# Expert 0's rows selected from contiguous columns, and matrices loaded chunk by chunk, in a hybrid backbone with routed experts

## The chip, the cores and the metric

One core of a Trainium2 chip runs the whole program. The metric is the time of one execution on the device in microseconds. The engines are named as in the profile: PE (TensorE, with PEld for its weight loads), DVE (VectorE), ACT (ScalarE), POOL (GpSimd) and SP (SyncE, which here only issues DMAs).

## What is computed

A step of a two-layer backbone for 512 sample tokens and 128 prompt tokens of width 1024. Each layer has a mixer with an output projection, a residual sum, a norm, and then a mixture of 16 experts, in which each expert chooses its tokens: 64 of the samples and 16 of the prompts. What matters here, with `norm` for the scaled norm and its modulation, and `x` the residual stream after the mixer:

```python
def ec_moe(x, router_w, w_gate, w_up, w_down):
    bsz, n_tok, _ = x.shape
    cap = n_tok * EC_CAPACITY // N_EXPERTS
    aff = jax.nn.softmax(jnp.einsum('btd,de->bte', x, router_w).astype(jnp.float32), axis=-1)
    gate, idx = lax.top_k(jnp.swapaxes(aff, 1, 2), cap)
    bidx = jnp.arange(bsz)[:, None, None]
    xe = x[bidx, idx]
    hid = jax.nn.silu(jnp.einsum('becd,edf->becf', xe, w_gate)) * jnp.einsum('becd,edf->becf', xe, w_up)
    ye = jnp.einsum('becf,efd->becd', hid, w_down) * gate[..., None].astype(x.dtype)
    return jnp.zeros_like(x).at[bidx, idx].add(ye)
```

In a layer: `x = x + g1 * out`, then `x = x + g2 * ec_moe(norm(x), ...)`. All is fp32. An expert has three matrices of 2 MB, so a layer reads 96 MB of weights.

## The kernel before

The kernel writes out the order of each engine by hand, in blocks; inside a block the engines meet at counting semaphores. `out_and_route` makes the block at issue for either layer, `experts` gives its second part. SBUF is full, so the same places are used by stages in turn.

**Output projection.** `product(t, h)` multiplies token tile t (tiles 0 to 3 are samples, PT = 4 is the prompts) by half h of the projection's 1024 columns. Each operand is split into a high and a low part of rounded fp32, so that a chunk k of the 8 chunks of the inner dimension takes three matmuls of 128x512 (L1663 to L1665). The high parts of the weights lie in `wv_high`, ring blocks 2 and 3, the low ones in `wv_low`, blocks 0 and 1. DVE adds the residual (L1730, L1732), ACT and DVE make the norm's factor `rstd`, and SP stores each tile of x and of the normed x in DRAM (L1638, L1640).

**Weights of the experts.** A matrix is loaded in four parts of 512 KB by `load_weights` (L1404) into one of ten slots, `wraw`, of which `SLOT_AT` tells the places. `EXPERT_ORDER` gives the order: gate 0, up 0, gate 1, up 1, down 0, gate 2, up 2, down 1 and so on, 48 matrices. The first three lie in places that are free early. Slots 3 to 6 are the four ring blocks, which the projection reads to its end. SP waits for its last product (`mm` at 10), issues matrices 3, 4 and 5, then waits for the logits and issues 6 and 7, then for the selection and issues 8, and last for the row stores and issues 9. From matrix 10 on, SP waits until the slot's former matrix is used up.

**Routing.** PE turns x (L1675) and multiplies it by the router (L1456). DVE makes the softmax and finds the eight largest of each row again and again (L1506 to L1509). PE turns the chosen slots (L1715, L1718), DVE merges the halves (L1755 to L1762) and gives the 64 token numbers of expert 0 as a column, `slot_of`. PE spreads it over the partitions (L1543), and DVE makes of it four matrices `pick` (L1809): 1 times the norm's factor where a token of tile t is the chosen one.

**Expert 0's rows.** The later experts fetch their rows by indirect DMAs on POOL (L1929, L1920). Expert 0's are made by matmuls from x in SBUF. `tensor_choice` multiplies each `pick` by x, with the columns regrouped: `columns` takes every eighth column, so that the chunk of rows that a transpose must turn lies together. Two column groups go to two array tiles of 64 columns (L1548), on which they make PSUM partitions 0 to 63 and 64 to 127. ACT copies the 128x512 sum (L2097), PE turns it with four transposes (L1971), ACT and DVE scale and shift it (L2066, L2134), and `first_hidden` multiplies chunk after chunk by the gate and up matrix (L1957 on four tiles of 32 columns). Between its chunks it does the prompts' choice (L1565 to L1567), the selection of the prompts' rows (L1558), and their turning (L1990). `keep_busy` (L143) are matmuls of the identity into a bank that nobody reads, between the selection and what follows.

**The other experts.** `into_hidden` (L1957, L1963), `turn_hidden` (L2023), `turn` (L1945) and `down` follow for each expert, and `down` waits for the weighing of the expert before (L2161, L2166). The last expert of layer 0 shares its time with what the next layer needs: `sync_last` issues three loads of its projection, `scalar_last` splits them on ACT (L2314) before ACT copies the last expert's weighed rows (L2120).

## Time and profile before

| | |
|---|---|
| median of 3 runs | 1416.8 us (1416.03 to 1419.14) |
| the profiled execution | 1415.48 us |
| its span, first to last instruction | 1413.6 us |
| mean granted TensorE clock | 0.982 |
| PE busy | 1324.3 us (94%) |
| DVE, ACT, POOL busy | 698.1, 529.4, 276.8 us |
| DMA | 333.80 MB; in the expert stages 369 to 388 GB/s in most slices |
| expert stage of layer 0 | about 443 to 741 us |
| expert stage of layer 1 | about 1098 to 1401 us |

The time is that of an execution as the host sees the device; the span leaves out what lies before the first and behind the last instruction. Each row of a timeline merges instructions of one form that follow each other. An fp32 matmul of the program is two rows of PE in the profile, two passes; a transpose is one. Ends of matmuls are modelled, so starts are the better clock, and a group's time is from its first start to its last end. A load's part in the landing time is not all transfer, since it queues behind what was issued before.

### The profile page before, as it was taken

How to read it: one execution, taken by the hardware profiler on the slowest of the kernel's cores; microseconds unless marked ns; L12 is line 12 of the kernel's file. 1: busy time of each engine (PE TensorE's matmuls, PEld its weight loads, DVE VectorE, ACT ScalarE, POOL GpSimd, SP SyncE). 2: the span in 40 equal slices, each digit the busy share in tenths (PEclk: the TensorE clock that was granted, in tenths of full speed). 3: DMA queues.
4: the chain of work that ended last, by engine and by line, in shares of the span. 5: the costliest groups of instructions: out<-in, count | busy, mean ns of one | idle time of the engine just before them, and what ended most of it. 6: DMA issues, size and time to landing. Idle time of an engine off the chain costs nothing. (4 is left out here: it accounts for less than half of the span.)

```text
span 1413.6 us, 27174 instructions
## 1 busy us (share of the span) xinstructions
PE 1324.3 (94%) x11105; PEld 806.2 (57%) x11105; DVE 698.1 (49%) x1636; ACT 529.4 (37%) x1221; POOL 276.8 (20%) x237
## 2 busy tenths in 40 slices
PE   5999998889899999999989999989899999999995
PEld 1756566766686444444438998555588444444443
DVE  1536514677635333344357628866735344333435
ACT  2723113676333322222225468665523322222213
POOL 0001104596002011111100040555301011111101
PEclk7999999999999999999999999999999999999997
DMA  9688860131437999999982022050053999999985
GB/s 364 232 327 333 331 217 25 37 144 46 182 119 258 369 374 374 375 374 376 388 294 77 4 69 60 1 223 1 14 225 112 373 378 376 374 375 379 374 312 179
DMA packets 105799, 333.80 MB, mean 236 GB/s; under 512 B 23182, under 2 KB 29164, under 8 KB 99532
## 3 DMA queue, kind: packets, MB, share of 16 engines
q1 hardware_dynamic: 99276, 310.11, 57.9%
q0 software_dynamic: 5824, 19.86, 6.0%
q8 instruction: 88, 1.44, 0.4%
q10 hardware_dynamic: 576, 2.10, 0.4%
q14 instruction: 35, 0.29, 0.1%
HBM read 308.13 MB, written 23.89 MB: 235 GB/s over the span
## 5 line engine op out<-in xcount | busy, mean ns | idle before, releaser
L1957 PE MATMUL psum<-wraw,proj 128*32 128x512 f32 x3072 | 403.0, 598 | 7.7 <-issue 6.0
L1963 PE MATMUL psum<-wraw,proj 128*16 128x256 f32 x3072 | 235.6, 381 | 0.6 <-ACT proj L2071 0.6
L1963 PEld LDWEIGHTS psum<-wraw,proj 128*16 128x16 f32 x3072 | 90.2, 97 | 232.2 <-issue 227.4
L1957 PEld LDWEIGHTS psum<-wraw,proj 128*32 128x32 f32 x3072 | 96.8, 110 | 79.7 <-issue 15.8
L1925 POOL DMA_INDIRECT x_rows<-modrow,idx x30 | 42.9, 1429 | 452.6 <-DVE modrow L2166 452.6
L2084 ACT ACTIVATE proj<-psum 128x320 f32<-128x320 f32 x32 | 14.0, 437 | 286.5 <-PE psum L2023 286.5
L2128 DVE TENSOR_SCALAR proj<-psum,proj 128x64 f32<-128x64 f32 x232 | 55.6, 312 | 107.0 <-PE psum L1945 107.0
L1336 POOL TENSOR_SCALAR ring<-ring,small 128x640 f32<-128x640 f32 x48 | 90.3, 1886 | 39.8 <-DVE small L1275 39.4
L2161 DVE SCALAR_TENSOR_TENSOR modrow<-psum,proj 64x512 f32<-64x512 f32 x60 | 45.0, 749 | 84.2 <-PE psum L1963 83.8
L2153 DVE TENSOR_TENSOR proj<-proj,psum 64x512 f32<-64x512 f32 x32 | 22.1, 690 | 127.5 <-ACT proj L2091 127.5
L1266 DVE TENSOR_REDUCE small<-psum 128x1 f32<-128x640 f32 (+1 forms) x80 | 57.3, 717 | 52.3 <-PE psum L1241 51.8
L421 PE MATMUL psum<-ring_rounded,xT_rounded 128*128 128x512 f32 (+1 forms) x200 | 76.6, 383 | 3.4 <-DVE xr_rounded L638 3.4
L423 PE MATMUL psum<-ring_rounded,xr_rounded 128*128 128x512 f32 (+1 forms) x200 | 74.0, 370 | 0.0
L422 PE MATMUL psum<-ring_rounded,xT_rounded 128*128 128x512 f32 (+1 forms) x200 | 73.9, 370 | 0.0
L2060 ACT ACTIVATE proj<-psum,proj 128x64 f32<-128x64 f32 x232 | 67.6, 398 | 16.3 <-PE psum L1945 16.1
L1663 PE MATMUL psum<-ring_rounded,proj_rounded 128*128 128x512 f32 x160 | 66.8, 418 | 1.8 <-DVE xT_rounded L1766 1.5
L1665 PE MATMUL psum<-ring_rounded,xT_rounded 128*128 128x512 f32 x160 | 64.4, 403 | 0.0
L1664 PE MATMUL psum<-ring_rounded,proj_rounded 128*128 128x512 f32 x160 | 64.1, 401 | 0.0
L1310 ACT ACTIVATE ring<-psum,small 128x640 f32<-128x640 f32 x64 | 50.9, 795 | 24.9 <-DVE small L1269 20.8
L2166 DVE SCALAR_TENSOR_TENSOR modrow<-psum,proj 16x256 f32<-16x256 f32 x120 | 57.8, 482 | 1.8
L2091 ACT ACTIVATE proj<-psum 64x512 f32<-64x512 f32 x32 | 18.8, 589 | 101.5 <-PE psum L1963 101.5
L1210 PE MATMUL psum<-ident,ring 128*128 128x128 f32 x320 | 46.3, 275 | 9.6 <-POOL ring L1336 7.0
(519 smaller groups left out, 2410.6 us busy)
## 6 DMA issues: line engine op xcount, KB each, us to landing
wraw<-in_exp_w_gate_dram SPq DMA_DIRECT2D x128, 512.0 KB, 16.4
wraw<-in_exp_w_up_dram SPq DMA_DIRECT2D x128, 512.0 KB, 16.8
wraw<-in_exp_w_down_dram SPq DMA_DIRECT2D x128, 512.0 KB, 16.5
ring<-in_ada_w_dram SPq DMA_DIRECT2D x29, 1024.0 KB, 6.9
hold<-in_ada_w_dram SPq DMA_DIRECT2D x14, 1024.0 KB, 6.8
ring<-in_ev_w_in_dram SPq DMA_DIRECT2D x4, 2048.0 KB, 12.3
xr<-x_rows SPq DMA_DIRECT2D x15, 512.0 KB, 7.5
proj<-in_ada_w_dram SPq DMA_DIRECT2D x5, 1024.0 KB, 9.1
```

The lines of the kernel that those rows point to most:

```text
L421: pe.matmul(bank(n % UB, w), xTh[:, k, tok], mv[:, k, :], start=(k == 0), stop=False)
L422: pe.matmul(bank(n % UB, w), xTh[:, k, tok], mv_low[:, k, :], start=False, stop=False)
L423: mm = pe.matmul(bank(n % UB, w), xTl[:, t, k, :], mv[:, k, :], start=False, stop=(k == KD - 1))
L1266: own.link(dve.tensor_reduce(mx[:, i % NB:i % NB + 1], scores(i), AX.XY if wide[i] else AX.X, ALU.max))
L1336: pool.tensor_scalar(Pb[u % NB][:, 0:w], Pb[u % NB][:, 0:w], rr[:, u % NB:u % NB + 1], None, ALU.mult).then_inc(s["n"], 1)
L1663: pe.matmul(bank(u % 4), xh[:, t % 2, k, :], wv_high[:, k, cut], start=(at == 0), stop=False)
L1664: pe.matmul(bank(u % 4), xh[:, t % 2, k, :], wv_low[:, k, cut], start=False, stop=False)
L1665: mm = pe.matmul(bank(u % 4), x_low, wv_high[:, k, cut], start=False, stop=(at == KD - 1))
L1957: mm = pe.matmul(psum[quad(q, 32), b, :], xs[:, quad(q % 2, 32)], pair[q // 2], start=first, stop=last)
L1963: mm = pe.matmul(psum[quad(q, CAPP), b, 0:QP], xs[:, CAPS:CAP], pair[q // 2][:, q % 2 * QP:(q % 2 + 1) * QP], start=first, stop=last)
L2060: ins = act.activation(xgT[:, e % 2, k, lo:hi], bank(0)[:, k * CAP + lo:k * CAP + hi], ACT.Identity, scale=scale_of[:, c, k:k + 1], bias=s ...
L2166: return dve.scalar_tensor_tensor(out=y[CAPS:CAP, q * QP:(q + 1) * QP], in0=psum[rows, 4, 0:QP], scalar=gd[rows, 1, e:e + 1], in1=g2p[rows ...
```

## The change

Three things change.

1. **The selection.** It takes contiguous columns of x. The two array tiles take two token tiles each (0 and 1; 2 and 3) in place of two groups of columns, for one half of the 1024 columns and then for the other, in two PSUM banks. Each tile thus has a sum over half of the samples. PE waits for all four picks first.
2. **The turning.** ACT copies each half's sums when they are ready. A product with `both_halves`, the upper and lower half of the identity side by side and summed (128x64), adds the two halves of the samples and turns the rows in one: eight fp32 products, of every eighth column as weights, into banks 5 and 6. The modulations read from there. The order of the chunks follows the banks. The prompts' sums go to bank 1 and the prompts' slots to bank 7.
3. **The loads.** The last product, now `last_product`, takes the chunks 4 to 7 first and tells after each chunk that it is done. After chunk i SP issues one part of each of two matrices (`free_chunk`): parts 0 to 3 of matrices 3 and 4 after the first four chunks, those of 5 and 6 after the last four. For that the slots of 4, 5 and 6 exchange their ring blocks. The last tile's store of the normed x is issued behind the parts of the first two chunks. The third load for the next layer waits for 47 matrices used and not 46, since its place is now that of matrix 46.

The diff, cut to its core:

```diff
-        SLOT_AT = [("ring", 4 * 4096), ("ring", 5 * 4096), ("proj", PROJ_SLOT), ("ring", 3 * 4096), ("ring", 2 * 4096), ("ring", 0), ("ring", 4096),
+        SLOT_AT = [("ring", 4 * 4096), ("ring", 5 * 4096), ("proj", PROJ_SLOT), ("ring", 3 * 4096), ("ring", 4096), ("ring", 2 * 4096), ("ring", 0),
...
                 sp.wait_ge(s["st"], 16 * ST)
-                load_weights(sp, l, 6, ready)
                 load_weights(sp, l, 7, ready)
-                sp.wait_ge(selected, 1)
+                sp.wait_ge(selected, 2)
...
                 keep_busy(pe, 2, 5)
-                for t in range(ST):
-                    pe.wait_ge(s["pick"], t + 1)
-                    for c in range(2):
-                        mm = pe.matmul(psum[64 * c:64 * c + CAPS, 1, :], pick[:, t, :], columns(t, 4 * c, 4 * c + 4), start=(t == 0), stop=(t == ST - 1))
-                    if t == ST - 2:
-                        turn_affinities(pe, 1)
-                mm.then_inc(selected, 1)
-                keep_busy(pe, 5, 5)
+                pe.wait_ge(s["pick"], ST)
+                for h in range(2):
+                    for j in range(2):
+                        for c in range(2):
+                            t = 2 * c + j
+                            mm = pe.matmul(psum[64 * c:64 * c + CAPS, h, :], pick[:, t, :], xr[:, t, h * 512:(h + 1) * 512], start=(j == 0), stop=(j == 1))
+                        if h == 1 and j == 0:
+                            turn_affinities(pe, 1)
+                    mm.then_inc(selected, 1)
+                keep_busy(pe, 5, 4)
+
+            def tensor_rows(pe, rows):
+
+                for k in range(KD):
+                    at = k // 2 * CAPS
+                    mm = pe.matmul(bank(5 + k % 2)[:, at:at + CAPS], rows[:, k::KD], both_halves, start=True, stop=True)
+                return mm
...
+            LAST_ORDER = (4, 5, 6, 7, 0, 1, 2, 3)
+
+            def free_chunk(sp, i):
+
+                sp.wait_ge(s["chunk"], i + 1)
+                for m in (3, 4) if i < 4 else (5, 6):
+                    load_part(sp, l, m, ready, i % 4)
...
                         sp.dma_start(x_rows[t * P:(t + 1) * P, :], xr[:, t, :]).then_inc(s["st"], 16)
+                        if t == ST - 1:
+                            for i in range(2):
+                                free_chunk(sp, i)
                         sp.wait_ge(s["xm"], t + 1)
                         sp.dma_start(xm_rows[t * P:(t + 1) * P, :], xm[:, t % 2, :]).then_inc(s[f"row{t % 2}"], 16)
-                    sp.wait_ge(s["mm"], 2 * TILES)
-                    load_weights(sp, l, 3, ready)
-                    load_weights(sp, l, 4, ready)
-                    load_weights(sp, l, 5, ready)
+                    for i in range(2, KD):
+                        free_chunk(sp, i)
...
+                    def last_product():
+
+                        b = bank((2 * PT + 1) % 4)
+                        pe.wait_ge(s["gx"], 2 * PT - 2)
+                        for at, k in enumerate(LAST_ORDER):
+                            pe.matmul(b, xh[:, PT % 2, k, :], wv_high[:, k, 512:], start=(at == 0), stop=False)
+                            pe.matmul(b, xh[:, PT % 2, k, :], wv_low[:, k, 512:], start=False, stop=False)
+                            mm = pe.matmul(b, xT_r[:, k * NT + PT * P:k * NT + (PT + 1) * P], wv_high[:, k, 512:], start=False, stop=(at == KD - 1))
+                            mm.then_inc(s["chunk"], 1)
...
+                            own(dve.tensor_tensor(both_halves, ident[:, 0:CAPS], ident[:, CAPS:2 * CAPS], ALU.add))
...
-                    pe.wait_ge(s["selc"], 1)
-                    for k in range(4):
-                        mm = pe.transpose(bank(k // 2)[:, k % 2 * P:(k % 2 + 1) * P], picked_s[:, k, :], ident[:, :])
-                    mm.then_inc(s["xT"], 2)
+                    pe.wait_ge(s["selc"], 2)
+                    routed["tensor_rows"](pe, picked_s).then_inc(s["xT"], 2)
...
-                act.wait_ge(s["sel"], 1)
-                act.activation(picked_s, bank(1).rearrange("p (k d) -> p k d", k=4), ACT.Copy).then_inc(s["selc"], 1)
+                for h in range(2):
+                    act.wait_ge(s["sel"], h + 1)
+                    act.activation(picked_s[:, h * 512:(h + 1) * 512], bank(h), ACT.Copy).then_inc(s["selc"], 1)
...
-                for i, used in enumerate((41, 43, 46)):
+                for i, used in enumerate((41, 43, 47)):
```

How the selection stands in PE's order, before (a row counts the program's matmuls, of 128 partitions of `xr` by 64 columns of picks into 64x512 sums; waits are left out):

```order
L143 MATMUL psum<-ident 128x128 x2
L1548 MATMUL psum<-xr,proj 64x512 x6
L1465 MATMUL psum<-ident,proj 16x128
L1548 MATMUL psum<-xr,proj 64x512 x2
L143 MATMUL psum<-ident 128x128 x5
L1971 MATMUL psum<-ident,proj 128x128 x4
```

and as the change has it:

```order
L143 MATMUL psum<-ident 128x128 x2
L1554 MATMUL psum<-xr,proj 64x512 x6
L1468 MATMUL psum<-ident,proj 16x128
L1554 MATMUL psum<-xr,proj 64x512 x2
L143 MATMUL psum<-ident 128x128 x5
L1564 MATMUL psum<-small,proj 128x64 x8
```

The selection keeps its 8 matmuls and its fillers; the four transposes became eight products.

On SP's queue in layer 0, from the last tile's stores on, before (wraw_61 is slot 3, wraw_64 slot 6):

```order
L1638 DMA x_rows<-xr 128x1024
L1640 DMA xm_rows<-xm 128x1024
L1404 DMA wraw_61<-in_exp_w_up_dram 128x1024 x4
L1404 DMA wraw_62<-in_exp_w_down_dram 128x1024 x4
L1404 DMA wraw_63<-in_exp_w_gate_dram 128x1024 x4
L1404 DMA wraw_64<-in_exp_w_up_dram 128x1024 x4
```

and as the change has it:

```order
L1658 DMA x_rows<-xr 128x1024
L1402 DMA wraw_61<-in_exp_w_up_dram 128x1024
L1402 DMA wraw_62<-in_exp_w_down_dram 128x1024
L1402 DMA wraw_61<-in_exp_w_up_dram 128x1024
L1402 DMA wraw_62<-in_exp_w_down_dram 128x1024
L1663 DMA xm_rows<-xm 128x1024
L1402 DMA wraw_61<-in_exp_w_up_dram 128x1024
L1402 DMA wraw_62<-in_exp_w_down_dram 128x1024
```

The store of the last normed tile stands behind four parts; the parts of two matrices alternate, and those of slots 5 and 6 follow in the same way.

## Rows read from the trace of the kernel before

**Rows 1.** Timeline, PE, one row an expert: start us, us, line, op, tiles, count.

```profile
679.34 0.71 PE L2023 MATMUL psum<-ident,proj 80*128 80x80 f32 x4
...
697.22 0.70 PE L2023 MATMUL psum<-ident,proj 80*128 80x80 f32 x4
```

**Rows 2.** The same in layer 1.

```profile
1334.78 0.71 PE L2023 MATMUL psum<-ident,proj 80*128 80x80 f32 x4
...
1351.93 0.71 PE L2023 MATMUL psum<-ident,proj 80*128 80x80 f32 x4
```

**Rows 3.** Waits of PE, 640 to 700 us: total, times, longest.

```profile
PE psum L1957 <- DMA wraw<-in_exp_w_up_dram: 0.5, 1, 0.5
```

**Rows 4.** Windows: PE, PEld, DVE, ACT, POOL busy, clock, DMA share, GB/s.

```profile
430.00:434.00 4.00, 4.00 (x20) 3.23 (x19) 3.72 (x15) 0.00 (x0) 1.78 (x2) 1.00 0.00 0
```

**Rows 5.** Timeline, SP's DMA issues, layer 0.

```profile
422.06 0.32 SPq L1640 DMA_DIRECT2D xm_rows<-xm  x1
434.00 1.76 SPq L1404 DMA_DIRECT2D wraw<-in_exp_w_up_dram  x4
```

**Rows 6.** Timeline, ACT: copies out of PSUM.

```profile
428.42 0.60 ACT L1855 ACTIVATE proj<-psum 128x512 f32<-128x512 f32 x1 [1.00 <-PE psum L1665]
434.01 0.60 ACT L1855 ACTIVATE proj<-psum 128x512 f32<-128x512 f32 x1 [4.99 <-PE psum L1665]
```

**Rows 7.** Timeline, PE, from the selection to the first expert product.

```profile
443.64 5.71 PE L1548 MATMUL psum<-xr,proj 128*64 128x512 f32 x12
...
449.49 2.03 PE L1548 MATMUL psum<-xr,proj 128*64 128x512 f32 x4
451.45 1.38 PE L143 MATMUL psum<-ident 128*128 128x128 f32 x10
452.67 0.60 PE L1971 MATMUL psum<-ident,proj 128*128 128x128 f32 x4
453.86 0.64 PE L1957 MATMUL psum<-wraw,proj 128*32 128x512 f32 x4 [0.59 <-ACT proj L2066]
```

**Rows 8.** Timeline, DVE: the four picks.

```profile
443.18 1.10 DVE L1809 TENSOR_SCALAR proj<-psum,small 128x64 f32<-128x64 f32 x4 [1.14 <-PE psum L1543]
```

**Rows 9.** Timeline, PE: groups that price one pass, layer 0.

```profile
438.27 1.04 PE L1675 MATMUL psum<-ident,xr 128*128 128x128 f32 x8
...
456.34 2.78 PE L1957 MATMUL psum<-wraw,proj 128*32 128x512 f32 x24
458.94 1.10 PE L1558 MATMUL psum<-xr,proj 128*32 128x256 f32 x8
...
463.40 1.92 PE L1963 MATMUL psum<-wraw,proj 128*16 128x256 f32 x32 [0.28 <-ACT proj L2071]
465.26 1.09 PE L1945 MATMUL psum<-ident,proj 64*128 64x64 f32 x8
```

**Rows 10.** Timeline, PE: two 64-column tiles, contiguous.

```profile
308.34 1.08 PE L1223 MATMUL psum<-proj 128*64 128x256 f32 x8
```

**Rows 11.** Timeline, PE: fp32 products with 128 columns of weights.

```profile
750.16 1.95 PE L2440 MATMUL psum<-small,xr 128*128 128x128 f32 x16
```

**Rows 12.** Timeline, POOL: gather of expert 1.

```profile
442.87 1.12 POOL L1929 DMA_INDIRECT proj<-xm_rows,idx  x1 [5.57 <-DVE idx L1762]
```

**Rows 13.** DMA issues, 440 to 470 us: KB each, median us to landing.

```profile
xm_rows<-xm ACTq DMA_DIRECT2D x1, 512.0 KB, 8.2
...
proj<-xm_rows,idx POOLq DMA_INDIRECT x3, 7.4
```

**Rows 14.** Timeline, ACT: what follows the last expert of layer 0.

```profile
731.22 7.04 ACT L2314 ACTIVATE ring_rounded<-ring 128x832 fp32r<-128x832 f32 x8 [4.58 <-DMA ring<-in_od_w_in_dram]
739.45 0.63 ACT L2120 ACTIVATE ring_rounded<-ring 80x512 fp32r<-80x512 f32 x1 [1.18 <-DVE ring L2161]
```

**Rows 15.** Windows with a lowered TensorE clock.

```profile
390.00:395.00 5.00, 5.00 (x18) 4.03 (x18) 0.98 (x3) 1.93 (x4) 0.00 (x0) 0.66 0.00 0
...
729.20:734.30 5.10, 5.10 (x33) 1.68 (x37) 2.73 (x7) 3.08 (x4) 1.40 (x1) 0.50 0.69 155
```

More of the change, by code:

```diff
@@ L1395, in build, with load_part, load_weights @@
         PARTS = 4
-        def load_weights(sp, l, m, ready):
+        def load_part(sp, l, m, ready, i):
             n, e = EXPERT_ORDER[m]
             src = A[EXPERT_W[n]][l, e].rearrange("(p k) n -> p (k n)", p=P)
-            parts = PARTS
-            w = 4096 // parts
-            for i in range(parts):
-                sp.dma_start(wraw[m % NSLOT][:, i * w:(i + 1) * w], src[:, i * w:(i + 1) * w]).then_inc(ready[m % NSLOT], 16)
+            w = 4096 // PARTS
+            sp.dma_start(wraw[m % NSLOT][:, i * w:(i + 1) * w], src[:, i * w:(i + 1) * w]).then_inc(ready[m % NSLOT], 16)
+        def load_weights(sp, l, m, ready):
+            for i in range(PARTS):
+                load_part(sp, l, m, ready, i)
         def landed(m):
@@ L1446, in out_and_route @@
             token_of, slot_of = small[:, 48:48 + TILES], small[0:CAPS, 56:57]
+            both_halves = small[:, 64:64 + CAPS]
             ssq, rstd, mxs, sums = small[:, 0:5], small[:, 8:13], small[:, 16:21], small[:, 24:29]
@@ L1557, in tensor_prompts @@
                 for q in range(4):
-                    mm = pe.matmul(psum[32 * q:32 * q + 2 * CAPP, 3, 0:256], pick_p, columns(PT, 2 * q, 2 * q + 2), start=True, stop=True)
+                    mm = pe.matmul(psum[32 * q:32 * q + 2 * CAPP, 1, 0:256], pick_p, columns(PT, 2 * q, 2 * q + 2), start=True, stop=True)
                 mm.then_inc(selected, 1)
@@ L1563, in tensor_chosen @@
                 for e in range(2):
-                    at = CAPS + CAPP * e
-                    pe.matmul(spread[:, at:at + CAPP], ident[0:NE, e:e + 1].to_broadcast([NE, P]), idxf[0:NE, CAPS:CAP], start=True, stop=True)
+                    pe.matmul(spread_p[:, e * CAPP:(e + 1) * CAPP], ident[0:NE, e:e + 1].to_broadcast([NE, P]), idxf[0:NE, CAPS:CAP], start=True, stop=True)
                 pe.transpose(bank(7)[0:CAP, 0:NE], idxf[0:NE, :], ident[0:NE, 0:NE])
@@ L1591, in vector_chosen @@
                 dve.wait_ge(s["it"], 4)
-                dve.tensor_scalar(pick_p, spread[:, CAPS:CAPS + 2 * CAPP], token_of[:, PT:TILES], rstd[:, PT:TILES], ALU.is_equal, ALU.mult).then_inc(s["pick"], 1)
+                dve.tensor_scalar(pick_p, spread_p, token_of[:, PT:TILES], rstd[:, PT:TILES], ALU.is_equal, ALU.mult).then_inc(s["pick"], 1)
                 dve.tensor_copy(idx[CAPS:CAP, :], bank(7)[CAPS:CAP, 0:NE]).then_inc(s["chosen"], 1)
@@ L1708, in _ @@
                     product(PT, 0, 7, KD)
-                    product(PT, 1)
+                    last_product()
                     keep_busy(pe, 20, 3)
@@ L1808, in _ @@
                     for t in range(ST):
-                        dve.tensor_scalar(pick[:, t, :], spread[:, 0:CAPS], token_of[:, t:t + 1], rstd[:, t:t + 1], ALU.is_equal, ALU.mult).then_inc(s["pick"], 1)
+                        dve.tensor_scalar(pick[:, t, :], spread, token_of[:, t:t + 1], rstd[:, t:t + 1], ALU.is_equal, ALU.mult).then_inc(s["pick"], 1)
                     then["vector"](dve, own)
@@ L1829, in turn_copy @@
                             act.wait_ge(s["turned"], 2 * t + h + 1)
-                            if h == 0:
+                            if h == 0 and t < PT:
                                 act.wait_ge(s["mm"], 2 * t + 2)
@@ L1975, in first_hidden @@
                     pairs = [[wraw[m][:, k * 512:(k + 1) * 512] for m in (0, 1)] for k in range(KD)]
-                    for n, k in enumerate((0, 4, 1, 5, 2, 6, 3, 7)):
+                    for n, k in enumerate((0, 2, 4, 6, 1, 3, 5, 7)):
                         if n < 3:
@@ L1987, in first_hidden @@
                         if n == 7:
-                            pe.wait_ge(s["selc"], 2)
+                            pe.wait_ge(s["selc"], 3)
                             for j in range(2):
-                                mm = pe.transpose(bank(j)[:, 0:P], picked_p[:, j, :], ident[:, :])
+                                mm = pe.transpose(bank(5 + j)[:, 0:P], picked_p[:, j, :], ident[:, :])
                             mm.then_inc(s["xT"], 2)
@@ L2183, in vector @@
                 dve.wait_ge(s["xT"], 2)
-                for k in (2, 6, 3):
+                for k in (1, 3, 5):
                     modulate_picked(k)
```

33 lines of the change are left out of this document (19 added, 14 removed).

## The prediction

> **What bounds the kernel now.** I read the windows of busy time and clock first, then the timeline of PE, then that of SP and the waits. In both expert stages PE has no idle window, and one expert takes 17.15 us from one turn of hidden rows to the next [rows 2]. PE sets the pace there: a stage begins with the first expert's products and ends 16 experts later. Once it doesn't. In layer 0 the step to expert 15 took 697.22 - 679.34 = 17.88 us [rows 1], 0.73 us more, and in that stretch PE waits for a DMA, an up matrix [rows 3]: the weight stream has just run out of lead. It is a second bound right behind the first, and a change that starts PE earlier gains only if the stream starts earlier too.
>
> The stream stands still before the stage: DMA share 0.00 from 430 to 434 us [rows 4]. SP, done with its last row store at 422.06, waits for the very last product and issues the fourth matrix at 434.00 [rows 5]. That product is the half that runs between the two PSUM copies, 428.42 to 434.01 [rows 6]: 5.59 us for 8 chunks, 0.70 each. What the first expert waits for is the selection: its matmuls begin at 443.64, filler at 451.45, the transposes at 452.67, the first expert product at 453.86 [rows 7].
>
> **Part one, the selection.** Before, it is 8 matmuls of 512 columns, two passes each, on two 64-column tiles side by side: 8 paired passes, from 443.64 to 451.45, 7.81 us [rows 7]. The moving operand steps 8 floats. Six pairs are listed with 5.71 us and the last two with 2.03, so a further pair costs (5.71 - 2.03) / 4 = 0.92 us, and 7.81 - 8 x 0.92 = 0.45 us go to the affinities' transpose among them and to the end. Afterwards it is again 8 paired passes, of contiguous columns. Price of one: four tiles do 24 contiguous passes of 512, six groups of four, in 2.78 us [rows 9], and one group by itself takes 0.64 [rows 7], so (2.78 - 0.64) / 5 = 0.43 us. Two 64-column tiles do four pairs of 256 contiguous columns in 1.08 us [rows 10], at most 0.27 a pair, so 0.54 for 512 is the upper end. It is the step of 8 floats that costs the double, not the tiles: four tiles take 1.10 us for 8 strided passes of 256, and 1.92 us for 32 contiguous ones, 0.48 for 8 [rows 9]. So 8 x 0.43 + 0.45 = 3.89 us, which is -3.92 (upper end -3.0).
>
> The change waits for all four picks before the first matmul. DVE makes four in 1.10 us [rows 8]. PE started 443.64 - 443.18 = 0.46 after their start, so it starts at least 1.10 - 0.46 = 0.64 later, and at most 1.10 less a quarter, 0.82; I take 0.76, since PE needs a little to hear of a pick. The affinities' transpose comes nearer to the picks, behind six paired passes, 2.6 us after the start. DVE makes the softmax that it needs right behind the picks, with seven operations on 16 columns and one exponent on ACT; it held nothing before, and I put it at 0.
>
> **Part two, the turning.** Four transposes (0.60 us [rows 7]) become 8 fp32 products with 128 weight columns and 64 moving ones, 16 passes. Such a group of 16 takes 1.95 us with contiguous weights [rows 11]. Here the weights step 8 floats. Low end: transposes of such weights take 1.09 us for 8, contiguous ones 1.04 [rows 9], a factor of 1.05. High end: the factor 1.10 / 0.48 = 2.3 that the moving operand paid, 4.5 us. I take 1.95, since a strided weight load is nearest to a strided weight load. +1.35 us; at the high end +3.9.
>
> The Trainium skill speaks against this part: page "SBUF — State Buffer", its passage on 16-byte cachelines, lets fp32 step by 4 elements at full rate and charges beyond, and it makes no exception for weights. By it the sum would be the first rival's, by the rows it is mine.
>
> The selected rows were copied once, 128x512 as in [rows 6], 0.60 us. Now the first half is copied while PE still multiplies, and the second takes the same 0.60 under the five fillers (1.38 us [rows 7]): 0. The modulations, the prompts' selection and their waits keep number and form and change banks: 0. The DVE addition that makes the summed identity is one small operation while PE multiplies without a gap: 0, and 0.2 us without that cover.
>
> A layer: -3.92 + 0.76 + 1.35 = -1.81 us; first product at 452.05.
>
> **Part three, the stream.** Chunk 1 of the last product ends at 428.4 + 0.7 = 429.1, so the fourth matrix starts 434.0 - 429.1 = 4.9 us earlier. On SP's queue the last row store moves from 422.06, idle DMA time, behind four parts of 512 KB: 512 KB more in the stream, at the page's 375 GB/s 1.4 us. Net lead +3.5 us. Layer 0 needs 1.81 + 0.73 = 2.54 us of it for PE to run through; the lead suffices by 1.0, and the 0.73 us go too. Layer 1 had no such wait. More lead is worth nothing: PE's pace holds.
>
> Who waits for the moved store? POOL's gather for expert 1, at 442.87 [rows 12]. Four issues take SP 1.76 us [rows 5], so the store is issued at about 430.9, and with the 8.2 us that one took amid traffic [rows 13] it lands at 439.1. Cover is left: 3.8 us, and after the gather's 7.4 us [rows 13] still 12 us until PE turns these rows at 465.26 [rows 9]. The third load for the next layer now waits for one down product more, about 5 us; ACT waits for it before it copies the last rows, after 731.22 + 7.04 = 738.26, with 1.18 us to spare [rows 14], and has the new lead. 0; without the lead about 1 us, once.
>
> **Sum.** 2 x -1.81 - 0.73 = -4.35 us. The profiled execution took 1415.5 us, with a span of 1413.6; it would be 1411.1. The median of the runs shown lies 1.3 us above it, and I forecast that: **1412.4 us**.
>
> **Rivals.** (1) *The strided weights pay* in full: 4.5 us instead of 1.95, so a layer gains -1.81 + 2.55 = +0.74; the wait in layer 0 still goes: 1416.8 + 1.5 - 0.7 = 1417.6, no change. Against it stand 1.09 and 1.04 [rows 9]; for it, that those were transposes of 64 rows and not products of 128. 11%.
> (2) *The stream comes no earlier where it counts*, because parts issued two by two and the store among them are served worse. At a lead of 0, PE gains nothing in layer 0 and under 1 us in layer 1: 1416. For it: [rows 3] shows the lead exhausted. Against: the DMAs stand quite still for 4 us [rows 4]. 8%.
> (3) *Slower, by the clock.* PE now stands about 0.7 us before the selection. The granted clock was 0.66 in 390 to 395, though PE was busy, and 0.50 in 729.2 to 734.3, after PE had stood for 3 us [rows 15]. Those 5.1 us of work at 1.2 GHz cost 2.6. One such fall a layer gives 1412.4 + 5.1 = 1417.5; it decides from 3.6 us lost a layer (2 x 3.6 - 4.35 = +2.8), and two falls, at the picks and at the copy, give 1412.4 + 10.2 = 1422.6. Against: PE stood 0.59 us before the first product [rows 7] without a fall there. One 4%, two 4%.
> (4) *More than forecast*: the 1.3 us between median and profiled run are waits for weights too, and go with the new lead: 1411.1 or less. 12%.
>
> **The numbers.** My own case has 59% and reaches from 1411.2 to 1414.0 (one bound of the selection or a quarter of the weights' price). 0.2%, 2.8 us, is about what a measurement of this kernel can tell from no change: below 1414.0 is faster. Faster: 59 + 12 + 2 of rival 2 = 0.73. Same: 11 + 6 + 4 = 0.21. Slower: 4 and 2 for what I don't see = 0.06. The range, 1410.2 to 1416.2, takes in part of rival 2 and half of rival 1's price, and leaves out their far ends and the clock.
>
> **What would show it.** The selection 3.9 us long; the turning 1.9 to 2.0 us for 16 passes; the first expert product 8.9 us after the picks start (before 453.86 - 443.18 = 10.7); the DMAs busy from 430 us; no expert of layer 0 at 17.9 us, all at 17.15. The forecast is wrong if the turning takes over 3 us, if PE waits for a weight DMA anywhere, if the granted clock around 444 us is under 1, or if more went than these two places show.

## The result: slower, and by how much

| | before | after |
|---|---|---|
| median of the runs | 1416.4 us (6 runs, 1414.1 to 1419.1) | 1427.0 us (6 runs, 1423.6 to 1430.0) |
| profiled execution, its span | 1415.5, 1413.6 us | 1424.7, 1422.9 us |
| mean granted TensorE clock of the profiled execution | 0.982 | 0.973 |
| the same over the runs | 0.980 (23 runs) | 0.970 (6 runs) |

The ratio is 1.0067, with a 95% interval of 1.0049 to 1.0085. The forecast was 1412.4 us, in a range of 1410.2 to 1416.2. The result is 10.6 us slower than before, outside the range, and on the side that I had given 6%.

### The profile page after: what moved, and what is told of

Read it like the earlier page. It is cut to its first block and busy times, and to the rows that moved or that the text cites. A ratio compares the mean times of both kernels' runs of the same rounds, so it can differ in the third digit from the quotient of the medians.

```text
span 1422.9 us, 27224 instructions
## 1 busy us (share of the span) xinstructions
PE 1336.5 (94%) x11129; PEld 818.9 (58%) x11129; DVE 698.2 (49%) x1638; ACT 529.5 (37%) x1223; POOL 276.4 (19%) x237
## 5 line engine op out<-in xcount | busy, mean ns | idle before, releaser
L1684 PE MATMUL psum<-ring_rounded,proj_rounded 128*128 128x512 f32 x144 | 59.8, 416 | 1.8 <-DVE xT_rounded L1797 1.5
L1686 PE MATMUL psum<-ring_rounded,xT_rounded 128*128 128x512 f32 x144 | 57.6, 400 | 0.0
L1685 PE MATMUL psum<-ring_rounded,proj_rounded 128*128 128x512 f32 x144 | 57.1, 397 | 0.0
```

Of the source, the lines that this page charges most:

```text
L1684: pe.matmul(bank(u % 4), xh[:, t % 2, k, :], wv_high[:, k, cut], start=(at == 0), stop=False)
L1685: pe.matmul(bank(u % 4), xh[:, t % 2, k, :], wv_low[:, k, cut], start=False, stop=False)
L1686: mm = pe.matmul(bank(u % 4), x_low, wv_high[:, k, cut], start=False, stop=(at == KD - 1))
```

## The profile after

I read the windows of the changed stretch first: from the first matmul of the selection to the first one of the prompts' rows, in layer 0 and layer 1. The columns are those of [rows 4]: the stretch, the busy time of PE, PEld, DVE, ACT and POOL with their instructions, the granted clock, the DMA share and GB/s. First the kernel before.

```profile
443.64:458.94 15.30, 14.71 (x79) 4.62 (x82) 5.47 (x27) 3.77 (x9) 1.28 (x2) 1.00 1.03 396
1099.08:1114.38 15.30, 14.71 (x79) 4.62 (x82) 5.47 (x27) 3.77 (x9) 1.08 (x2) 1.00 1.03 392
```

And the changed kernel.

```profile
443.24:461.12 17.88, 17.29 (x90) 8.45 (x93) 4.77 (x24) 4.19 (x9) 0.93 (x1) 0.81 1.03 393
1104.66:1123.67 19.01, 18.42 (x89) 8.90 (x93) 4.77 (x24) 4.07 (x9) 0.91 (x1) 0.73 1.03 394
```

The forecast made this stretch 2.6 us shorter (-3.92 and +1.35). It became 2.58 us longer in layer 0 and 3.71 in layer 1. Two columns say why. The weight loads (PEld, the second one) are busy for 8.45 and 8.90 us where they were for 4.62. And the granted clock is 0.81 and 0.73 where it was 1.00.

The timeline of PE shows the places (start, length, line, operation, operands, count, and the idle time ahead with what ended it). Layer 0 first, then layer 1.

```profile
443.24 4.49 PE L1554 MATMUL psum<-xr,proj 128*64 128x512 f32 x12 [0.62 <-DVE proj L1841]
...
447.87 1.08 PE L1554 MATMUL psum<-xr,proj 128*64 128x512 f32 x4
...
450.10 3.91 PE L1564 MATMUL psum<-small,proj 128*128 128x64 f32 x16
454.59 3.37 PE L1993 MATMUL psum<-wraw,proj 128*32 128x512 f32 x16 [0.59 <-ACT proj L2100]
...
458.52 2.78 PE L1993 MATMUL psum<-wraw,proj 128*32 128x512 f32 x24
```

```profile
1104.66 2.80 PE L1554 MATMUL psum<-xr,proj 128*64 128x512 f32 x12 [0.62 <-DVE proj L1841]
...
1107.60 1.08 PE L1554 MATMUL psum<-xr,proj 128*64 128x512 f32 x4
...
1109.82 3.96 PE L1564 MATMUL psum<-small,proj 128*128 128x64 f32 x16
1114.38 3.64 PE L1993 MATMUL psum<-wraw,proj 128*32 128x512 f32 x16 [0.59 <-ACT proj L2100]
...
1119.04 4.80 PE L1993 MATMUL psum<-wraw,proj 128*32 128x512 f32 x24
```

In layer 1 the selection runs at full clock. Its 12 and 4 instructions start at 1104.66 and end at 1108.68, 4.0 us, against [rows 7] with 7.8: part one did what was forecast. In layer 0 the same 12 take 4.49 us instead of 2.80, since the clock fell to 1.2 GHz within them. The 16 passes of the turning take 3.91 and 3.96 us in both layers, where 1.95 was forecast from [rows 11]. The first product's rows show the second fall: 16 instructions in 3.37 and 3.64 us, and in layer 1 the 24 behind them in 4.80, where [rows 9] has 2.78. At full clock the 16 take 1.92 us (experiment 1, below). Ahead of both places PE stands idle for a short time: 0.62 us for the picks, which is new, and 0.59 us for the modulated rows, which stood in [rows 7] too, without a fall.

The stream did what was forecast. SP issues the fourth matrix at 428.01 ([rows 5]: 434.00), the DMAs are busy from 430 us ([rows 4]: share 0.00), and the expert that took 17.88 us [rows 1] takes 17.15. Of the 6.0 us between the two issues 1.1 are that this whole execution was ahead there: POOL's addition for the residual, which nobody changed, starts at 428.09 where it was 429.20. That leaves the 4.9 us of the forecast.

```profile
428.01 0.33 SPq L1402 DMA_DIRECT2D wraw<-in_exp_w_up_dram  x1
```

```profile
430.00:434.00 4.00, 4.00 (x25) 3.46 (x24) 3.69 (x14) 0.60 (x1) 1.17 (x2) 1.00 0.99 325
```

```profile
664.37 0.71 PE L2057 MATMUL psum<-ident,proj 80*128 80x80 f32 x4
...
681.52 0.71 PE L2057 MATMUL psum<-ident,proj 80*128 80x80 f32 x4
```

So in the profiled pair the span grows by 9.3 us: 2.58 + 3.71 = 6.3 in the changed stretches, 2 x 0.62 = 1.2 for the waits ahead of them, -0.73 for the stall that is gone. That makes 6.8. The other 2.5 us lie in code that did not change. These are windows of the kernel before and of the changed kernel behind layer 0's experts and in the attention of layer 1.

```profile
740.00:757.00 17.00, 11.76 (x71) 10.33 (x70) 12.15 (x23) 10.73 (x23) 3.35 (x5) 1.00 0.71 210
918.00:945.00 27.00, 22.54 (x119) 15.84 (x117) 16.22 (x47) 17.50 (x41) 14.30 (x9) 1.00 0.75 292
```

```profile
740.00:757.00 17.00, 13.15 (x62) 11.20 (x62) 11.34 (x21) 10.24 (x22) 3.35 (x5) 0.80 0.69 211
918.00:945.00 27.00, 24.05 (x103) 16.76 (x101) 11.23 (x33) 14.39 (x32) 10.15 (x7) 0.75 0.73 287
```

The clock fell there too, to 0.80 and 0.75 on average, though nothing was changed. Whether the change caused that is the question of experiment 5.

## The experiments

Each time stands beside runs of the kernel before on the same chip, whose median was 1415.6 us beside experiments 1 to 4 (23 runs), 1416.7 beside 5 to 8 (35) and 1417.6 beside 9 to 12 (29); a time is compared with its own. Each ratio is uncertain by 0.0013 to 0.0020 either way, which is 2 to 3 us. The stretch named above is what I compare in the profiles, since nearly all that changed lies in it.

**1. Regrouped rows.** The two copies on ScalarE write the chosen rows by their k, so that the turning reads neighbouring columns.

```diff
-                    mm = pe.matmul(bank(5 + k % 2)[:, at:at + CAPS], rows[:, k::KD], both_halves, start=True, stop=True)
+                    mm = pe.matmul(bank(5 + k % 2)[:, at:at + CAPS], rows[:, k * P:(k + 1) * P], both_halves, start=True, stop=True)
...
-                    act.activation(picked_s[:, h * 512:(h + 1) * 512], bank(h), ACT.Copy).then_inc(s["selc"], 1)
+                    act.activation(picked_s.rearrange("p (k d) -> p k d", k=KD)[:, :, h * 64:(h + 1) * 64], bank(h).rearrange("p (d k) -> p k d", k=KD), ACT.Copy).then_inc(s["selc"], 1)
```

> The changed kernel, with ScalarE's two copies writing expert 0's rows regrouped, so that each turning product reads 128 neighbouring columns as weights instead of every eighth. Weights theory (the stride costs the PE about 0.13 us a pass, which made the turning 3.91 and 3.96 us where 1.95 was forecast): the 16 passes take 1.7 to 2.0 us in each layer, two layers give back 4 us, and with all the falls of the clock left as they are the time is about 1423. Rival, the size of the product sets it: the turning stays at 3.9 us and the time at 1427. Rival, the clock: the falls at 444, 454, 744, 925 and 1113 us cost the most (5 to 8 us in all); if they hang on the turning, they go and the time is 1414 to 1418; if not, 1421 to 1425 with falls in the same stages. The regrouped copies should cost the same as before, within 0.1 us; if a strided read of PSUM costs more, the 1.1 us from the last selection matmul to the turning grow.

Measured: 1417.3 us (1414.1 to 1422.4, 11 runs), ratio to before 1.0007 (0.9995 to 1.0020), mean clock 0.975. Its timeline of PE in layer 0:

```profile
446.57 4.49 PE L1554 MATMUL psum<-xr,proj 128*64 128x512 f32 x12 [0.62 <-DVE proj L1841]
...
453.43 1.90 PE L1564 MATMUL psum<-small,proj 128*128 128x64 f32 x16
455.92 1.92 PE L1993 MATMUL psum<-wraw,proj 128*32 128x512 f32 x16 [0.59 <-ACT proj L2100]
```

The turning takes 1.90 us. The weights theory holds: 2.0 us a layer. The stretch, by its windows:

```profile
446.57:460.99 14.42, 13.83 (x89) 6.26 (x93) 4.77 (x24) 4.20 (x9) 0.93 (x1) 0.88 1.03 391
1104.54:1117.26 12.72, 12.13 (x89) 5.93 (x93) 4.77 (x24) 4.09 (x9) 0.91 (x1) 1.00 1.03 387
```

Against the changed kernel it lost 3.46 us in layer 0 and 6.29 in layer 1, together 9.7; the medians, each against its own runs of before, differ by 8.9. 4.0 of that are the stride, the rest is the clock: no fall is left in layer 1, and in layer 0 the one at the selection alone, behind the same 0.62 us of idle time. The copies kept their 0.60 us.

**2. Selection and turning alone**, with the old order of slots and the old loads (the parts of the diff that touch `load_part`, `free_chunk`, `last_product` and `SLOT_AT` undone).

> Parts one and two of the change alone: the new selection and the new turning, with the weights asked for as in the kernel before (whole matrices behind the prompt's last product, the old order of the slots). If the loss comes from the turning and the clock in these parts: slower than before, 1425 to 1430, with the stall of 0.73 us at the twelfth expert of layer 0 there in part or whole, and falls of the clock at the selection. If the asking chunk by chunk is what brought the loss: 1412 to 1416, as my sum for these two parts with a turning of 3.9 us gives it (1416.4 - 3.6 + 4 = 1417).

Measured: 1427.5 us (1421.8 to 1429.7, 6 runs), ratio 1.0075 (1.0058 to 1.0092), mean clock 0.970. The whole loss comes with these two parts. The stretch is the same to 0.03 us as in the changed kernel:

```profile
447.23:465.08 17.85, 17.26 (x89) 8.43 (x93) 4.77 (x24) 4.19 (x9) 0.93 (x1) 0.81 1.03 399
1108.59:1127.60 19.01, 18.43 (x89) 8.89 (x93) 4.76 (x24) 4.07 (x9) 0.91 (x1) 0.73 1.03 398
```

No expert takes over 17.15 us behind the first step in either layer, although the loads are the old ones: PE comes late enough for the stream to keep up. My expectation had the stall still there.

**3. The loads alone**, the counterpart: the old selection and turning.

> Part three alone: matrices 3 to 6 asked for chunk by chunk, the old selection and the old turning. Forecast: the stall of 0.73 us in layer 0 goes and the stream is 5 us ahead, so 1412.5 to 1416. If the asking disturbs something (a queue, the clock in the odd layer at 744 and 925 us): 1419 to 1425 with those falls there and none at the selection.

Measured: 1420.7 us (1415.8 to 1422.7, only 5 runs), ratio 1.0037 (1.0024 to 1.0050), mean clock 0.975. The stall is gone and the stretch takes 15.3 us in both layers, as before, yet the time is above before. I had it repeated, below.

**4. Regrouped rows and fillers.** Experiment 1 with filler products over both idle times.

```diff
-                keep_busy(pe, 2, 5)
+                keep_busy(pe, 5, 5)
...
                     routed["tensor_rows"](pe, picked_s).then_inc(s["xT"], 2)
+                    keep_busy(pe, 3, 4)
```

> As the run with regrouped rows, with three more filler products before the selection (over the 0.62 us in which the PE waits for the picks) and three behind the turning (over the 0.59 us in which it waits for the modulated rows). Clock theory, idle time before a stretch of half-width products makes the clock fall: the falls around 444 and 454 us, and in layer 1 at the same places, are gone, and the time is 3 to 5 us below the run without fillers. Rival, the falls come with the products themselves (64 of 128 columns of the array): they stay, and the time is the same within 1 us. Falls in the odd layer at 744 and 925 us, whose code is unchanged: if they vary from kernel to kernel with no pattern, they are a matter of when the program passes there.

Measured: **1411.0 us** (1407.4 to 1416.4, 12 runs), ratio 0.9962 (0.9946 to 0.9978), mean clock 0.981. It beats the kernel before by 4.6 us, and the changed one, each against its own runs of before, by 15.

```profile
444.31:457.09 12.78, 12.78 (x96) 6.52 (x99) 4.76 (x24) 4.07 (x9) 0.93 (x1) 1.00 1.03 390
1103.44:1116.22 12.78, 12.78 (x96) 6.52 (x99) 4.77 (x24) 4.07 (x9) 0.91 (x1) 1.00 1.03 383
```

The stretch takes 12.78 us in both layers at full clock, 2.52 less than before: the -2.57 of the forecast (-3.92 + 1.35), once the weights are contiguous and the clock stays.

**5. The kernel before, profiled again.**

> The kernel before, unchanged, for a second profile of it and for the clock of more of its executions. Its first profile shows no fall of the clock at 742 and 923 us, where four or five of the others do, on the same code and behind the same idle times (2.46 us at 740, 1.8 us at 921). If these falls come by chance, this profile has one or both and the mean clock of the executions stays at 0.980 (time 1415.6); if they come with the change, this one has none again.

Measured: 1417.7 us (1414.5 to 1425.0, 12 runs), ratio 1.0013 (0.9997 to 1.0029), mean clock 0.979. The profiled execution was one of the longer ones, 1422.9 us, and its windows of the stages with unchanged code read

```profile
740.00:757.00 17.00, 12.23 (x48) 10.20 (x48) 10.28 (x18) 9.51 (x19) 3.35 (x5) 0.70 0.73 216
918.00:945.00 27.00, 24.89 (x112) 17.74 (x110) 9.69 (x27) 14.80 (x32) 8.21 (x6) 0.75 0.66 257
```

with a clock of 0.70 and 0.75. So the falls in those places are not the change's: they come in some executions of the kernel before as well. They go with the spread of single executions of one kernel, up to 10 us, and are why only the changed stretch can be compared between two profiles.

This profile has a fall at the changed place too, though the old selection has no wait of 0.62 us ahead: in layer 1 the clock is low from the fillers on and for the first 2.2 us of the selection. It is the only one among the eight stretches with the old selection (two each of the two profiles of the kernel before and of experiments 3 and 6). It hardly costs: the stretch takes 15.34 us instead of 15.30 and the 12 instructions 5.76 instead of 5.71 [rows 7].

```profile
1106.41:1121.75 15.34, 14.75 (x78) 4.82 (x81) 4.96 (x25) 3.59 (x8) 0.91 (x1) 0.93 1.03 393
```

```profile
1106.41 5.76 PE L1548 MATMUL psum<-xr,proj 128*64 128x512 f32 x12
```

The strided selection takes nearly the same time at either clock, while the contiguous one goes from 2.80 to 4.49 us. Part of what the new selection gains it can therefore lose to a fall that the old one did not feel.

**6. The loads alone, again**, the same kernel as in 3.

> The asking chunk by chunk alone, a second time: the first gave 1420.7 from 5 executions (1415.8 to 1422.7), which at their mean clock of 0.975 is 4 us above the kernel before instead of 3.5 below. If that was the chance of five executions: 1413 to 1416.5 with a clock of 0.979 to 0.980. If the loads do cost clock: 1419 to 1422 at 0.975 again.

Measured: 1418.1 us (1414.2 to 1422.0, 12 runs), ratio 1.0006 (0.9990 to 1.0021), mean clock 0.977. The 5 us of the first run were in part the chance of five executions. What is left is no gain where 0.73 us were forecast for this part alone, which is less than these runs can tell, and a clock slightly under that of before. This stays open, see below.

**7. The changed kernel with the fillers**, its weights still strided (the edit of 4 in the changed kernel).

> The changed kernel with its strided weights, and the six filler products of the run with fillers. The turning stays at 3.9 us (2.0 us a layer over the regrouped rows: 1411.0 + 4.0 = 1415). If the waits alone make the clock fall: no fall within 30 us behind the selection in either layer, 1414 to 1416.5. If the slow turning itself makes it fall: falls behind it at about 454 and 1113 us as in the changed kernel, 1418 to 1422.

Measured: 1418.3 us (1413.8 to 1420.6, 12 runs), ratio 1.0000 (0.9985 to 1.0016), mean clock 0.978.

```profile
445.89:460.69 14.80, 14.80 (x96) 8.54 (x99) 4.77 (x24) 4.08 (x9) 0.93 (x1) 1.00 1.03 384
1101.12:1115.92 14.80, 14.80 (x96) 8.54 (x99) 4.77 (x24) 4.08 (x9) 0.91 (x1) 1.00 1.03 391
```

14.80 us in both layers, without a fall. The slow turning is in there in full (PEld 8.54) and does not bring the clock down by itself. So it needs the waits. Against experiment 4 it is 2.02 us longer in the stretch: the price of the stride again. The median is still 1.8 us above the upper end of what I had expected without a fall.

**8. Regrouped rows and fillers, with the old loads.**

> New selection with regrouped rows and the fillers, but the weights asked for as before (whole matrices behind the last product). With the chunks this kernel took 1411.0. If the chunks are worth what was forecast (3.5 us, the stall of 0.73 us at the twelfth expert of layer 0 among them): 1414 to 1415. If they cost what the run with the chunks alone says (4 us and more): 1405 to 1408. If neither, 1410 to 1412.

Measured: 1418.3 us (1412.7 to 1424.0, 12 runs), ratio 1.0011 (0.9994 to 1.0028), mean clock 0.979. The stretch takes 12.79 us as in 4, but all of it is lost again: PE waits for the up matrices, in layer 0 and then in layer 1 (the waits of PE, total, times, longest), and the steps from 643.53 to 661.05 and on to 679.36 take 17.52 and 18.31 us.

```profile
PE psum L1970 <- DMA wraw<-in_exp_w_up_dram: 2.7, 4, 1.0
```

```profile
PE psum L1970 <- DMA wraw<-in_exp_w_up_dram: 1.7, 3, 0.8
```

```profile
643.53 0.71 PE L2035 MATMUL psum<-ident,proj 80*128 80x80 f32 x4
...
661.05 0.71 PE L2035 MATMUL psum<-ident,proj 80*128 80x80 f32 x4
...
679.36 0.70 PE L2035 MATMUL psum<-ident,proj 80*128 80x80 f32 x4
```

That is the worth of part three: nothing while PE is late, and 6.2 us once the selection is as fast as it should be (1.6 us above its own runs of before here, 4.6 below in experiment 4). I had expected 3.5.

**9 and 10. Fillers ahead of the selection only, and behind the turning only**, both in the changed kernel (one line each of the edit in 4).

> The changed kernel with three more fillers ahead of the selection only, so that the PE does not idle for 0.62 us before it; the strided turning and the 0.59 us behind it stay. With all six fillers the stretch from the selection to the prompts' rows had no fall of the clock and took 14.8 us; without any, 17.9 us (6.8 at the lower clock) and 19.0 us (10.2). If the wait ahead starts the falls and the rest follows from it: no fall in the stretch, 14.7 us in both layers, time 1416 to 1419. If the slow turning with its idle time behind it does so by itself: a fall of 3.4 us or more at the first product in both layers, 16 to 17 us, time 1421 to 1425.

> The counterpart: three fillers behind the turning only; the wait of 0.62 us ahead of the selection stays. If the wait ahead matters by itself: a fall within the selection in layer 0 (at full clock its first 12 instructions take 2.8 us, with the fall 4.5) and none at the first product. If neither: 14.8 us, as with all six. Time 1417 to 1423.

Measured: ahead only 1420.2 us (1414.0 to 1423.4, 12 runs), ratio 1.0013 (0.9995 to 1.0030); behind only 1421.6 us (1415.0 to 1425.8, 12 runs), ratio 1.0024 (1.0004 to 1.0044). The two medians don't tell them apart; the profiles do. Ahead only:

```profile
448.98:463.71 14.73, 14.14 (x90) 7.95 (x93) 4.77 (x24) 4.08 (x9) 0.93 (x1) 1.00 1.03 392
1104.16:1118.89 14.73, 14.14 (x90) 7.95 (x93) 4.77 (x24) 4.08 (x9) 0.91 (x1) 1.00 1.03 393
```

Behind only:

```profile
443.82:461.94 18.12, 18.12 (x95) 9.57 (x99) 4.77 (x24) 4.19 (x9) 0.93 (x1) 0.81 1.03 394
1102.38:1120.51 18.13, 18.13 (x96) 9.31 (x100) 4.77 (x24) 4.19 (x9) 0.91 (x1) 0.81 1.03 394
```

With the picks' wait covered the stretch has no fall, though PE still stands 0.59 us before the first product. With that wait open it has a clock of 0.81 in both layers, though the other is covered. So in these profiles, one of each kernel, it is the 0.62 us ahead of the selection that start the falls, given the slow turning behind; with contiguous weights (experiment 1) the same wait was followed by a fall in one layer of two. My expectation for the second run, that the first product would then be free of a fall, was wrong: its first 16 instructions took 2.96 and 3.16 us instead of 1.92, with filler just ahead of them.

```profile
455.84 2.96 PE L1993 MATMUL psum<-wraw,proj 128*32 128x512 f32 x16
```

```profile
1114.19 3.16 PE L1993 MATMUL psum<-wraw,proj 128*32 128x512 f32 x16
```

The fall at the first product therefore doesn't need the 0.59 us. What goes with it is the slow turning: in layer 0 of experiment 1, with contiguous weights, the fall at the selection is there and the one at the first product is not.

**11. Strides of the weights.** In the kernel before, the 20 fillers ahead of the prompt's turning become 20 products with the normalized rows as weights.

```diff
-                    keep_busy(pe, 20, 3)
+                    for gap in (1, 2, 4, 8):
+                        for n in range(5):
+                            pe.matmul(bank(3, P), xr[:, 0, 0:gap * P:gap], ident[:, :], start=True, stop=True)
```

> The kernel before, with its 20 fillers ahead of the prompt's turning replaced by 20 products of the same size whose weights are columns of the normalized rows at a distance of 1, 2, 4 and 8 elements, five each: it measures the price of the stride by itself. If the price is one of how far apart the 4-byte elements lie: 0.112 us a pass at distance 1, more at 2 and 4, 0.24 us at 8. If it is a step beyond 16 bytes: as at 1 for distances 2 and 4, 0.24 us at 8 alone. If the other operand or the short product made the turning slow: 0.112 us at all four. The time of the kernel stays at 1416 to 1420.

The kernel took 1424.3 us in its one run; the products are 2.6 us longer than the fillers, twice. Windows of that line alone, each over the ten passes of one distance (busy PE, busy PEld, clock, DMA share, GB/s; the counts take in neighbours that overlap):

```profile
432.87:433.98 1.11, 1.11 (x10) 1.11 (x10) 1.00 0.00 0
433.98:435.18 1.20, 1.20 (x12) 1.20 (x11) 1.00 0.83 198
435.18:437.51 2.33, 2.33 (x12) 2.33 (x11) 1.00 1.01 373
437.51:439.91 2.40, 2.40 (x11) 2.37 (x10) 1.00 1.02 374
```

A pass takes 0.111, 0.120, 0.233 and 0.240 us at a distance of 1, 2, 4 and 8 elements, at full clock. None of the three expectations is quite right: it is one step, and it lies between 2 and 4 elements. The DMAs are idle in the first window and busy in the others; that they don't matter is shown by experiment 1, where contiguous passes take 0.11 us at a DMA share of 1.03. The page "SBUF — State Buffer" of the Trainium skill, its passage on 16-byte cachelines, has fp32 step by 4 elements for free; here 4 elements, which is 16 bytes, already pay in full. The same passage wants two hits on each line of 16 bytes for full bandwidth. That rule fits the rows: a distance of 2 still has two elements on a line and 4 has one.

**12. Wait for each pick.** Experiment 4 without the fillers ahead: VectorE makes the picks in the order in which the selection takes them.

```diff
-                keep_busy(pe, 5, 5)
-                pe.wait_ge(s["pick"], ST)
+                keep_busy(pe, 2, 5)
...
+                            if h == 0:
+                                pe.wait_ge(s["pick"], 2 * j + c + 1)
...
-                    for t in range(ST):
+                    for t in (0, 2, 1, 3):
```

> The run with regrouped rows and fillers, without the three fillers ahead of the selection: instead VectorE makes the picks in the order 0, 2, 1, 3 and the selection waits for each as it comes to it. The wait of 0.62 us (0.67 of fillers) should shrink to under 0.1 us in each layer, with no fall of the clock in the selection: 1409.5 to 1411 where that run took 1411.0. If DMAs for the experts' matrices have no slack left, a stall comes back and it stays at 1411; if short waits between the first products let the clock fall: 1412 to 1415.

Measured: 1411.1 us (1410.3 to 1420.7, 12 runs), ratio 0.9961 (0.9942 to 0.9980), mean clock 0.982, like experiment 4. The idle time is gone without filler (no wait for the picks among PE's waits), and the stretch takes 12.98 and 13.86 us:

```profile
443.83:456.81 12.98, 12.98 (x97) 7.23 (x100) 5.47 (x27) 4.25 (x10) 1.28 (x2) 1.00 1.03 388
1095.00:1108.86 13.86, 13.86 (x96) 6.81 (x99) 4.96 (x25) 4.19 (x9) 0.91 (x1) 0.92 1.03 389
```

The 0.92 in layer 1 belongs to a fall that had begun before the selection. The expected gain over experiment 4 is under 1 us and doesn't show in the median.

**13. Transposes against products**, since the row that misled me was one of transposes. The same place as in 11, five groups of four: transposes of 128, 64 and 80 rows, then products of 128 and of 64.

```diff
-                    keep_busy(pe, 20, 3)
+                    for rows, product in ((P, False), (64, False), (80, False), (P, True), (64, True)):
+                        for k in range(4):
+                            w = xr[0:rows, 0, k::KD]
+                            if product:
+                                pe.matmul(bank(3, rows), w, ident[0:rows, 0:rows], start=True, stop=True)
+                            else:
+                                pe.transpose(bank(3, rows), w, ident[0:rows, 0:rows])
```

> The kernel before, its 20 fillers ahead of the prompt's turning replaced by five groups of four, all with weights at a distance of 8 elements (32 bytes): transposes of 128, 64 and 80 rows, then products of 128 and of 64 rows. The experts' rows are turned by transposes of 64 and 80 rows with just this distance at 0.11 us a pass, and that was the row that my forecast trusted. If the kind of instruction decides (a transpose passes its weights once and free of the price): 0.11 us a pass for all three groups of transposes, 0.24 us for both groups of products. If the number of rows decides: 0.24 us for 128 rows, 0.11 us for 64 and 80, whichever the kind. If both: 0.11 us for all but the products of 128 rows.

```profile
433.08 1.78 PE L1716 MATMUL psum<-ident,xr 128*128 128x128 f32 x12
434.70 4.17 PE L1714 MATMUL psum<-ident,xr 128*128 128x128 f32 x16
```

```profile
434.70:436.70 2.00, 2.00 (x8) 1.89 (x8) 1.00 0.97 324
436.70:438.60 1.90, 1.90 (x9) 1.89 (x8) 0.69 1.00 379
```

Its one execution took 1424.9 us, beside one of 1417.0 of the kernel before. The twelve transposes start within 434.70 - 433.08 = 1.62 us, 0.11 each and 0.15 more at each of the two changes of size, whatever the rows; the eight passes of the four products with 128 rows take 2.0 us, 0.24 each and something for the change to the next group. The four of 64 rows need as long a pass, 1.90 us for eight, though part of that is at the lower clock. So the kind of instruction decides: a transpose passes strided weights at full pace, an fp32 product pays.

## Why the prediction was wrong, point by point

- **The selection, -3.92 us a layer: right.** At full clock it takes 4.0 us (3.89 forecast) where it took 7.81.
- **Waiting for all picks, +0.76 us: right in size (0.62 us of idle time), wrong in what it does.** It was priced as time alone. Experiments 9 and 10 show that it starts the falls of the clock: the stretch takes 14.7 us when it is covered and 18.1 when it isn't.
- **The turning, "16 passes at 1.95 us", +1.35: the step that failed first.** The size was 3.91 and 3.96 us, near the high end of 4.5. I chose the low end, "since a strided weight load is nearest to a strided weight load", by the 1.09 and 1.04 us of [rows 9]. Experiment 13 shows what was not alike: those are transposes, these are products, and only products pay. The Trainium skill spoke against this part (page "SBUF — State Buffer", its passage on 16-byte cachelines), and the trace agrees with it at this distance: 0.24 us a pass where contiguous weights take 0.11. It was priced as the first rival, 1417.6 us at 11%.
- **The clock, rival (3), 8%: the step that failed second and costs more.** The mechanism was named with its place, the idle time before the selection, and argued away by the 0.59 us in [rows 7] that had no fall behind them. That was no evidence for the new place: experiment 10 has the new idle time alone and falls in both layers, experiment 9 has the old one alone and doesn't. What tells the two places apart the runs don't show. Experiment 1 shows that the two failed steps are not independent: with contiguous weights only one of the three places with a fall is left. In the changed stretch the clock costs 17.88 - 14.73 = 3.2 us and 19.01 - 14.73 = 4.3 (the 14.73 from experiment 9), near the 2.6 to 5.1 a layer that the rival had.
- **Rivals as alternatives.** The stride and the clock came together: +4.0 and +7.4 us on the 1412.4 make 1423.8. I had priced each alone, and my range took in half of one and nothing of the other. Both hang on the same stretch of PE, so they should have been priced as a pair too.
- **The stream, "4.9 us earlier": right.** 428.01 in place of 434.00, no step of 17.88 us. That PE needs it only if it is early was right as well, and experiments 2 and 8 show both sides of it: no stall with the old loads at a late PE, 5.8 us of longer steps at an early one (3.5 in layer 0, 2.3 in layer 1, all steps together). That layer 1 has no such wait, as I wrote, holds only for the old selection. The store and the gather behind the parts held nobody up.
- **What the sum leaves open.** 1416.4 + 6.3 + 1.2 - 0.7 is 1423.2, and 1427.0 was measured, 3.8 us more. The same sum, each from its own runs of before, leaves 5.1 us over with selection and turning alone (1422.4 against 1427.5), 4.6 with regrouped rows (1412.7 against 1417.3), 5.8 and 2.1 in the two of the loads alone, 2.0 and 3.1 in experiments 7 and 9. Nothing is over in experiments 4 and 8 (1411.2 against 1411.0 in 4), and 10 and 12 lie 2 us under it. Since each time is uncertain by 2 to 3 us, only what is well over 3 us is more than noise. The mean clock of all that have something over is low (0.970 to 0.978, the kernel before has 0.978 to 0.980), which speaks for more time at the lower clock, but experiment 8 reaches its sum at 0.979 and experiment 10 at 0.976. In which stage it lies one profile of each can't say, since stages with unchanged code have falls in some executions and not in others. I didn't settle it.

## What to carry to other kernels

Price a strided operand by a row of the same operand and the same kind of instruction; where products read strided fp32 weights, have the copy that writes them regroup them, which cost nothing here and gave back 2 us a layer. A new wait of PE, even one of 0.62 us, is also a question to the clock, so cover it with filler or split it by what is needed first, and compare only stretches whose code differs. Judge a part together with the parts that it serves: the earlier loads showed no gain alone, and 6.2 us with the fast selection.

## What the runs showed of the hardware that I had not expected

- Strided fp32 weights: 0.111, 0.120, 0.233 and 0.240 us a pass of a product at distances of 1, 2, 4 and 8 elements; transposes of 64, 80 and 128 rows at 8 elements 0.11 us.
- An idle time of 0.62 us was enough to be followed by a fall of the granted clock to 1.2 GHz: in seven of the eight stretches profiled with it (two each of the changed kernel, of experiments 1, 2 and 10), in none of the eight where filler covered it (experiments 4, 7, 8 and 9), and in one of the eight with the old selection. In two of the seven the fall came only near the end of the turning, some 8 us after the wait.
- Strided operands took nearly the same time at either clock: the old selection's 12 instructions 5.71 us at full clock and 5.76 with 2.2 us of it at 1.2 GHz. The contiguous selection took 2.80 and 4.49.
- The mean granted clock of executions of one and the same kernel runs from 0.972 to 0.985 (kernel before, 12 runs of experiment 5), and the time follows it, from 1425.0 down to 1414.5 us. The two profiles of that kernel have falls in different stages.
